# A home of their own for four raw chunks, normalised chunks two steps ahead, and 27 matmuls on zeroes ahead of the first product

## What is computed

```python
def first_block(...):
    h = jnp.concatenate([meta, x], axis=1)            # 272 positions
    hn = rmsnorm(h, mix_norm_g[l])
    proj = hn @ w_in[l]                               # cq, ckv, k_pe, q, k, v of the attentions
    ...                                               # two attentions, w_out, gated MLP with a conv
    h = h + conv_glu(rmsnorm(h, ffn_norm_g[l]), w_gate[l], w_up[l], ..., w_down[l])

def second_block(x, c, ...):
    mod = c_act @ w_ada[l] + b_ada[l]
    h = rmsnorm_2(x, norm_mix_g[l]) * (1.0 + sc_m) + sh_m
    proj = h @ w_in[l]                                # q, f, i, g of the recurrence, then the rest
    ...                                               # recurrence, conv, w_o, gated MLP, last norm
```

## Time and profile before

| | |
|---|---|
| median of 3 runs | 2638.06 us (2637.4 to 2638.41) |
| the profiled execution: its own time, its span | 2638.51 us, 2637.2 us |
| TensorE busy | 2591.6 us |
| VectorE busy | 1826.1 us |
| ScalarE busy | 1264.4 us |
| GpSimd busy | 337.6 us |
| mean granted TensorE clock | 0.995 of full speed |

### The profile page before, as it was taken

The page is one execution under the profiler, slowest core; times in us unless marked ns, Lnnn a source line. Parts: engine busy times, 40 slices in busy tenths (PEclk is TensorE's granted clock), DMA queues, the critical chain, the costliest instruction groups (busy, mean ns, idle before and its releaser), DMA issues.

```text
span 2637.2 us, 51391 instructions
## 1 busy us (share of the span) xinstructions
PE 2591.6 (98%) x21966; PEld 2565.4 (97%) x21966; DVE 1826.1 (69%) x2652; ACT 1264.4 (48%) x1989; POOL 337.6 (13%) x533
## 2 busy tenths in 40 slices
PE   8999999999999999999999999999999999999998
PEld 7988899999999999999999999999999999999998
DVE  8545477788878888888887667777887554455554
ACT  6666665544434444445444443345554443344443
POOL 4111001011111111231000001111221000000001
PEclk9999999999999999999999999999999999999999
DMA  7433455687898888885444578887768656565553
GB/s 224 140 109 105 125 175 180 224 277 266 280 289 279 280 266 276 271 293 192 153 153 159 192 235 283 277 285 234 255 222 285 206 186 198 197 195 195 189 188 126
DMA packets 500260, 571.18 MB, mean 217 GB/s; under 512 B 26880, under 2 KB 473600, under 8 KB 500032
## 3 DMA queue, kind: packets, MB, share of 16 engines
q1 hardware_dynamic: 468000, 463.77, 54.0%
q0 software_dynamic: 31600, 103.77, 12.1%
q10 hardware_dynamic: 432, 0.36, 0.0%
HBM read 565.74 MB, written 2.54 MB: 215 GB/s over the span
## 4 chain that ended last, share of the span: by engine, by line
PE 88%; DVE 5%; ACT 4%; issue 1%; DMA 1%; POOL 0%; SPq 0%; DVEq 0%; ACTq 0%
PE ps L745 27%; PE ps L746 27%; PE ps L747 27%; DVE wl L1877 2%; ACT wh L1355 1%; PE ps L871 1%; PE ps L713 1%; PE ps L714 1%; PE ps L715 1%; PE ps L1043 1%; DMA raw<-in_w_in 1%; DVE nx L1994 0%; PE ps L889 0%; PE ps L844 0%; ACT lp L1533 0%
## 5 line engine op out<-in xcount | busy, mean ns | idle before, releaser
L1877 DVE TENSOR_TENSOR wl<-raw,wh 128x1024 fp32r<-128x1024 f32 (+1 forms) x894 | 1059.9, 1201 | 525.1 <-ACT wh L1355 522.2
L1355 ACT ACTIVATE wh<-raw 128x1024 fp32r<-128x1024 f32 (+1 forms) x894 | 882.5, 1029 | 559.2 <-PE ps L747 551.4
L745 PE MATMUL ps<-xs,wh 128*128 128x256 f32 x2848 | 795.1, 279 | 3.3 <-DVE xs L1971 3.3
L746 PE MATMUL ps<-xs,wh 128*128 128x256 f32 x2848 | 788.7, 277 | 0.0
L747 PE MATMUL ps<-xs,wl 128*128 128x256 f32 x2848 | 788.6, 277 | 0.0
L745 PEld LDWEIGHTS ps<-xs,wh 128*128 128x128 f32 x2848 | 535.7, 188 | 4.7 <-DVE wl L1877 3.7
L746 PEld LDWEIGHTS ps<-xs,wh 128*128 128x128 f32 x2848 | 535.7, 188 | 1.0 <-issue 1.0
L747 PEld LDWEIGHTS ps<-xs,wl 128*128 128x128 f32 x2848 | 536.0, 188 | 0.0
L745 PE MATMUL ps<-xf_near,wh 128*128 128x258 f32 (+1 forms) x1408 | 395.3, 281 | 0.0
L747 PE MATMUL ps<-xf_near,wl 128*128 128x258 f32 (+1 forms) x1408 | 394.4, 280 | 0.0
L745 PE MATMUL ps<-hid,wh 128*128 128x256 f32 x1408 | 389.6, 277 | 0.0
(11 more groups left out here) (400 smaller groups left out, 3615.8 us busy)
## 6 DMA issues: line engine op xcount, KB each, us to landing
raw<-in_w_in SPq DMA_DIRECT2D x116, 1024.0 KB, 5.4
ada_raw<-in_w_ada POOLq DMA_DIRECT2D x384, 256.0 KB, 4.9
raw<-in_w_gate SPq DMA_DIRECT2D x44, 1024.0 KB, 6.2
raw<-in_w_up SPq DMA_DIRECT2D x44, 1024.0 KB, 5.9
raw<-in_w_ffn_gate SPq DMA_DIRECT2D x44, 1024.0 KB, 5.1
raw<-in_w_ffn_up SPq DMA_DIRECT2D x44, 1024.0 KB, 5.2
raw<-in_w_down SPq DMA_DIRECT2D x32, 1024.0 KB, 6.6
raw<-in_w_ffn_down SPq DMA_DIRECT2D x32, 1024.0 KB, 5.6
```

The source lines that it names most:

```text
L745: pe.matmul(dst, h[:, c, o:o + w], moving(g, 0, k), start=(k == 0), stop=False)
L746: pe.matmul(dst, h[:, c, o:o + w], moving(g, 1, k), start=False, stop=False)
L1355: act.activation(wh[i % NS][:, part], raw[i % NR][:, part], ACT.Copy).then_inc(s_hi, 1)
L1877: dve.tensor_tensor(wl[i % NS][:, part], raw[i % NR][:, part], wh[i % NS][:, part].bitcast(F32), ALU.subtract).then_inc(s_lo, 1)
```

## The change

Three things. The raw chunks 12 to 15 of `N_MIX2` get a tile `raw_late` behind `masks32`, in the place that `hid` covers until the last down product has been multiplied; `RAW_SHARED` loses these four chunks; and their shift columns, written at down product 1 before, are written at down product 7, behind the addition of that product's result. The semaphore counts follow: `gemm_raw` of `N_MIX2` waits for 3 on `s_shl` and not for 2. `SCALE_AT[N_MIX2]` moves each chunk one to three steps ahead, most of them two. And TensorE gets 27 matmuls of 256 columns, float32 by float32, on a tile that DVE sets to zero first, ahead of the first product, into a PSUM bank that is overwritten later.

```diff
-RAW_SHARED = {N_IN: [], N_FFN1: [], N_MIX2: list(range(6, 16)), N_FFN2: []}
+RAW_SHARED = {N_IN: [], N_FFN1: [], N_MIX2: list(range(6, 12)), N_FFN2: []}
...
-            N_MIX2: [10, 11, 12, 14, 16, 18, 19, 20, 21, 21, 22, 23, 24, 24, 25, 26],
+            N_MIX2: [8, 9, 10, 12, 14, 16, 18, 18, 19, 19, 20, 21, 21, 22, 22, 23],
...
-        masks32, _ = at("masks32", [P, nmask], F32, oo_home)
+        masks32, off = at("masks32", [P, nmask], F32, oo_home)
+        raw_late, off = at("raw_late", [P, 2, 4, T - Q0], F32R, off)
+        assert off <= mid
...
-                return raw_mix[:, h, i, :] if i < 6 else xx[:, h, i, Q0:T]
+                return raw_mix[:, h, i, :] if i < 6 else raw_late[:, h, i - 12, :] if i >= 12 else xx[:, h, i, Q0:T]
...
                 if NORM_SHIFT[n]:
-                    pe.wait_ge(s_shl, 2 if n == N_MIX2 else 4)
+                    pe.wait_ge(s_shl, 3 if n == N_MIX2 else 5)
...
+            pe.wait_ge(s_idle, 1)
+            for _ in range(27):
+                pe.matmul(PX[0][:, 0:SEQ], nx[0][:, 0:P], nx[0][:, 0:SEQ], start=True, stop=True)
             gemm_raw(N_IN, ("cq", 0))
...
                             if g == 1:
                                 act.wait_ge(s_gain, 2)
-                                raw_shift_hi(N_MIX2)
+                                raw_shift_hi(N_MIX2, slice(0, 2))
+                            if g == 7:
+                                raw_shift_hi(N_MIX2, slice(2, 3))
                             raw_his(N_MIX2, RAW_LAG[N_MIX2].get(g, []))
...
+            dve.memset(nx[0][:, 0:SEQ], 0.0).then_inc(s_idle, 1)
             dve.wait_ge(s_gain_in, 16)
...
                             if g == 1:
-                                raw_shift_lo(N_MIX2)
+                                raw_shift_lo(N_MIX2, slice(0, 2), 2)
+                            if g == 7:
+                                raw_shift_lo(N_MIX2, slice(2, 3), 3)
                             raw_lows(N_MIX2, RAW_LAG[N_MIX2].get(g, []))
```

More of the change, by code:

```diff
@@ L532, in raw_shift @@
             if n == N_MIX2:
-                parts = [raw_mix[:, h, :, 0:META - Q0], xx[:, h, 6:KD, Q0:META]]
+                parts, cuts, c = [raw_mix[:, h, :, 0:META - Q0], xx[:, h, 6:12, Q0:META], raw_late[:, h, :, 0:META - Q0]], (0, 6, 12, KD), 0
             else:
[L535 to L538, removed]
+                parts, cuts, c = [x[:, h, :, 0:META - Q0] for x in raw_ffn], (0, 8, KD), 48
+            return [(x, mod[:, c + a:c + b].unsqueeze(2).to_broadcast([P, b - a, META - Q0])) for x, a, b in zip(parts, cuts, cuts[1:])]
         def root_of(n):
@@ L594, in build @@
         s_cst2 = sem("rest_of_cst_landed")
+        s_idle = sem("idle_operand_set")
         s_lpool = [sem(f"lane_squares_added{j}") for j in range(2)]
@@ L1417, in raw_his, with raw_shift_hi @@
                         act.activation(raw_body(n, 0, i), raw_src(n, i), ACT.Copy, scale=norm_gain(n, i)).then_inc(s_rh, 1)
-            def raw_shift_hi(n):
+            def raw_shift_hi(n, part=slice(None)):
                 act.wait_ge(s_mod, 4 if n == N_MIX2 else 16)
-                for x, c in raw_shift(n, 0):
+                for x, c in raw_shift(n, 0)[part]:
                     act.activation(x, c, ACT.Copy).then_inc(s_shh, 1)
@@ L1928, in raw_lows, with raw_shift_lo @@
                                                  op0=ALU.mult, op1=ALU.subtract).then_inc(s_rl, 1)
-            def raw_shift_lo(n):
-                dve.wait_ge(s_shh, 2 if n == N_MIX2 else 4)
-                for (x, c), (h, _) in zip(raw_shift(n, 1), raw_shift(n, 0)):
+            def raw_shift_lo(n, part=slice(None), his=5):
+                dve.wait_ge(s_shh, his)
+                for (x, c), (h, _) in list(zip(raw_shift(n, 1), raw_shift(n, 0)))[part]:
                     dve.tensor_tensor(x, c, h.bitcast(F32), ALU.subtract).then_inc(s_shl, 1)
```

## The result

| | kernel before | changed kernel |
|---|---|---|
| median of the runs | 2638.23 us (10 runs, 2636.32 to 2640.8) | 2644.5 us (10 runs, 2641.41 to 2646.81) |
| ratio to before | 1 | 1.0025, 95% interval 1.0017 to 1.0033 |
| profiled execution: own time | 2638.51 us | 2643.89 us |
| profiled execution: span | 2637.2 us | 2642.6 us |

The kernel became slower, by some 6.6 us by the ratio (4.5 to 8.7 by its interval; the two medians are 6.3 apart).

What follows compares the result with a forecast made beforehand. TensorE, busy nearly all the span at full clock, was taken as the bound, leaving only idle times and slow stretches to win; 3.2 + 3.4 + 1.5 - 2.3 - 1.5 = +4.3 on 2638.1 gave 2642.4 us, range 2638.0 to 2645.0.

Steps and rivals of the forecast that it cites:

- Part 1: Start of the kernel: 27 float32 matmuls on zeroes end at 14.8 us, not 9.65; 5.1 late, 1.9 regained: +3.2 us.
- the prediction's bounds: Start: TensorE's low-clock time lies between some 2 and 6 us, so the calls end at 13.6 to 15.6, +2.1 to +4.1.
- Rival A: Start: calls on zeroes may cost half the sums' price and end by 9.65; -0.9 replaces +3.2, 2638.3 us; chance 0.12.
- calls that end in time: Start: were the 27 over by 9.65, the later slab halves would limit the win to 0.9 us of the 1.9.
- Part 2: Start of `q`: TensorE waits for the third `s_shl` write, +3.4 us of idling, and one slow clock stretch behind it, +1.5.
- Part 3: Mixer's `g`: earlier scaling cuts 3.3 us of idling to 1.0, -2.3, and removes the slow clock stretch after 1235, -1.5.
- Chunks 8 and 12 are then in time by more than 2 us: Mixer's `g`: the low parts behind the former 3.3 us of idling no longer delay TensorE; chunk 14 is late next.
- Rival C: Mixer's `g`: chunk 14 is late enough that the clock falls as before, 2.5 us more, 2644.9 us; chance 0.13.
- The sum: Whole kernel: 3.2 + 3.4 + 1.5 - 2.3 - 1.5 = +4.3 us on the profiled execution's 2638.5.
- Theory 1: Whole kernel: each part costs what it moves: calls 0.43 us each, `q` wait 3.4 and low stretch, norm gives some 3 back.
- theory 2: Between 56 and 300 us: the surplus over the forecast is additional low clock stretches that come and go with any shift.
- The median shares the rest: Whole kernel: the median of the runs, 0.4 us under the profiled execution at 2638.1, moves by the same +4.3 us.

## Why the prediction was right, and where it was off

**Part 1, the price of the 27 calls (+3.2 forecast): right.** The first trace shows +2.84 at the reciprocal; the four traces with 27 calls have it at 36.65 to 37.62, mean 37.09, which is 3.2 above the mean of the five without any (33.91). The changed kernel's stretches before its first product:

```profile
1.20:5.00 3.80, 3.80 (x10) 3.12 (x11) 0.00 (x0) 1.70 (x3) 0.00 (x0) 1.00 0.78 243
5.00:14.40 9.40, 9.40 (x46) 8.26 (x45) 7.30 (x13) 8.35 (x17) 1.48 (x1) 1.00 1.10 366
```

The clock column says 1.00 for both, because the trace's record of the clock begins with its rise, at 4.6 us here, and what lies ahead of it counts as full clock. The starts of the single instructions tell the level: they lie 0.427 us apart up to 4.3 and 0.216 behind 4.7, two to a call, so 0.85 and 0.43 us a call, where the forecast had 0.86 and 0.43. The clock rose at 4.6, 5.1, 5.5 and 6.5 us in the four traces, and the calls took 13.58, 13.86, 14.02 and 14.54 us: half a microsecond more for each microsecond that it rose later, as the prediction's bounds had it. Rival A, a call at half the price, is excluded.

In time the calls cost 3.7 and 5.3 us by the two pairs that differ in them alone, ±2.3 us each. What they have over 3.2 agrees with the additional low time that the runs' mean clocks show. The prediction's estimate for calls that end in time, 0.9 us, compares with 0.7 at the reciprocal for 13 calls, and with nothing measurable in the medians.

**Part 2, the wait at `q` (+3.4 and +1.5): right.** 3.34 us of idling, by the chain that was forecast, and a low stretch of 3.4 us that costs 1.45. Moving the wait to chunk 12 takes 4.2 to 4.8 us off. That the stretch follows was right for this trace but is no rule: with 54 calls the same idling had none behind it. The prediction expected the view to name DVE `raw_late` for the wait; it says "issue".

**Part 3, the norm ahead (-2.3 and -1.5): the direction right, one step wrong.** The step that failed is "Chunks 8 and 12 are then in time by more than 2 us", for which the prediction gave no working. It holds for 8, but chunk 12 is 0.68 us late. All chunks are scaled before `i` is read out and chunk 12's high part is made by then too, but its low part stands on DVE behind the read-out and a half slab, as the rows above show and as the list in "The change" had it. The earlier steps push that read-out back: it came 2.6 us behind the start of `g` before, was forecast at 3.8, and came at 4.4 (1236.16 - 1231.75).

That chunk 14's wait is 1.04 us, where 1.0 was forecast, is luck. Its low part was forecast at 10.5 us behind the start of `g` and ended at 11.7 (1243.41); the wait is short because TensorE had already lost 0.68 us at chunk 12. Together `g` idles for 1.72 us and not for 1.0. The low stretch in `g` did go, for its 1.5 us (1.6 between two traces that differ in it). Rival C didn't come about in this trace; with the later wait alone, 2.01 us of idling did have a low stretch behind it.

**The sum (+4.3)** came out as +5.3 in the profile and +6.6 (4.5 to 8.7) in the runs. By the table of the result the 1.0 in the profile is -0.4 for the calls, +0.1 for the wait, +0.5 for the norm, and 0.8 for a piece that the sum didn't have: between 36 and 1190 us the changed kernel's execution had seven low stretches, that of before four. The second trace of the same kernel had two, and a time as long, so the number in a single trace explains little. Theory 1 accounts for most of the change; that the runs with 27 calls have a lower mean clock is theory 2's share of it, 1 to 2 us. The sum of the parts in the runs, about 4.5 for the calls, 4.5 for the wait and -2.9 for the steps, is 6.1, and the rest is below what the intervals resolve. "The median shares the rest" was the step that was too confident: the profiled executions stand up to 3.1 us from the median of their version, and 4.8 with 54 calls.

The forecast was for no measurable change, on the slow side (0.68); what came, slower by over 0.2%, had 0.29. The time lies in the range with 0.5 us to spare, and that upper edge was set there for rival C, which is not what happened.

**What the change wanted to do** is to be had more cheaply: the step numbers alone give -2.9 us, with chunk 14's low part moved one place -4.2 (ratio 0.9984, 0.9975 to 0.9993; the two can't be told apart in the runs), and neither the home of their own nor the calls on zeroes add anything measurable to that.

## What to carry to other kernels

Filler work on TensorE must be priced by the kernel's own rows of that type and size, and must end before the operands arrive: every call past that point was paid in full here, while the whole prize was some 0.7 us in the traces and nothing measurable in the medians. Where a buffer is split, look at which wait covers its new part: a wait set ahead of the first chunk for a write that only chunk 12 needs cost 3.3 us of idling and a low stretch, and moving it took 4.2 to 4.8 us off, though chunk 12 was then late by 0.7 to 2.0 us in `g`, where it had been 0.7. Before memory is spent on freeing a place early, check when its next writer gets to it: here it got there after the last reader had gone.

## What the runs showed of the hardware that was not expected

Whether a wait of TensorE is followed by a low stretch is not settled by its length: 3.3 us of idling near 57 us and at `q` had 6.8, 3.4 or 0 us at half clock beginning in it or behind it in different executions, and the traces of two versions have no low stretch between the start and the end of the span. A stretch of 3.4 us cost 1.4 to 1.6 us in `q` and `g`, and about 0.5 us between 36 and 1190 us, where TensorE meets waits for other engines soon after. Versions with 27 calls on zeroes ahead of their first product had a lower mean clock over the whole span than those without; the cause stays open.
